# One decoder layer: work taken off VectorE, the way into the recurrence reordered, and a norm by ln and exp

## What is computed

```python
def rms_norm(x, gain):
    y = x * lax.rsqrt(jnp.mean(x * x, axis=-1, keepdims=True) + EPS)
    return y * gain
...
def step(S, inp):                       # one chunk of the recurrence, 8 heads
    qc, kc, vc, lc = inp
    b = jnp.cumsum(lc, axis=2)
    o = jnp.einsum('bhtd,bhde->bhte', qc * jnp.exp(b), S)
    ...
    o = o + jnp.einsum('bhts,bhse->bhte', a, vc)
    S = jnp.exp(b_last)[..., None] * S + jnp.einsum('bhsd,bhse->bhde', kc * jnp.exp(b_last[:, :, None] - b), vc)
...
def mixer_out(o_att, o_hg, og, attn_gain, hg_gain, w_out, dtype):
    a = rms_norm(o_att.reshape(B, T, ATT_WIDTH), attn_gain)
    h = rms_norm(o_hg, hg_gain).reshape(B, T, HG_WIDTH) * jax.nn.silu(og)
    return jnp.concatenate([a, h], axis=-1) @ w_out
```

## Time and profile before

| | |
|---|---|
| median of 3 runs | 2861.77 us (2860.55 to 2863.96) |
| time of the profiled execution | 2865.61 us, span 2863.9 us |
| TensorE busy | 2788.0 us (97%) |
| VectorE busy | 1472.6 us (51%) |
| ScalarE busy | 1007.2 us (35%) |
| GpSimd busy | 89.5 us (3%) |
| granted TensorE clock, mean | 0.988 |

### The profile page before, as it was taken

How to read it: one execution, slowest core, us unless ns; L and a number is a source line. 1 busy time by engine, 2 the same in 40 slices (tenths; PEclk the granted TensorE clock), 3 DMA queues, 4 the chain that set the end, 5 groups by cost and what they waited for, 6 DMA issues and landing times.

```text
span 2863.9 us, 50898 instructions
## 1 busy us (share of the span) xinstructions
PE 2788.0 (97%) x20916; PEld 2672.8 (93%) x20916; DVE 1472.6 (51%) x1854; ACT 1007.2 (35%) x1150; POOL 89.5 (3%) x161
## 2 busy tenths in 40 slices
PE   7999999999999999999999998999999999999999
PEld 5779999999999999998887787799999999999999
DVE  3434444434444444456666678875444434444433
ACT  3434333222233233333332344444333223222222
POOL 1110000000000010100000000020000000000000
PEclk9999999999999999999999998999999999999999
DMA  6365555455555454643336643445554456555454
GB/s 225 89 202 147 149 146 169 132 150 167 152 152 148 127 163 147 221 142 108 116 112 207 213 157 127 152 139 173 156 146 143 135 148 177 146 146 146 131 150 138
DMA packets 631369, 436.23 MB, mean 152 GB/s; under 512 B 14605, under 2 KB 615869, under 8 KB 623998
## 3 DMA queue, kind: packets, MB, share of 16 engines
q1 hardware_dynamic: 627746, 417.25, 48.2%
q0 software_dynamic: 2384, 14.11, 1.4%
q10 hardware_dynamic: 1100, 2.91, 0.3%
HBM read 421.16 MB, written 21.32 MB: 154 GB/s over the span
## 4 chain that ended last, share of the span: by engine, by line
PE 91%; DVE 5%; ACT 2%; issue 2%; DMA 0%; SPq 0%; POOLq 0%; POOL 0%; ACTq 0%; DVEq 0%
PE bank L409 65%; PE bank L763 12%; PE bank L1767 2%; PE bank L687 2%; PE bank L689 2%; PE bank L688 2%; ACT whi L742 1%; PE bank L1387 1%; DVE ors_h L2007 1%; DVE wlo L747 1%; PE bank L1175 1%; PE bank L1333 1%; ACT sc L1251 0%; PE bank L1176 0%; PE bank L1191 0%
## 5 line engine op out<-in xcount | busy, mean ns | idle before, releaser
L314 DVE TENSOR_TENSOR wlo<-wraw,whi 128x2048 fp32r<-128x2048 f32 (+1 forms) x305 | 612.7, 2009 | 508.9 <-ACT whi L310 486.0
L310 ACT ACTIVATE whi<-wraw 128x2048 fp32r<-128x2048 f32 (+1 forms) x305 | 513.3, 1683 | 679.2 <-PE bank L409 679.2
L409 PE MATMUL bank<-xl,whi 128*128 128x320 f32 x2816 | 441.8, 309 | 0.0
L409 PE MATMUL bank<-xh,whi 128*128 128x320 f32 x2816 | 441.8, 309 | 0.0
L409 PE MATMUL bank<-xh,wlo 128*128 128x320 f32 x2816 | 441.6, 309 | 0.0
L409 PEld LDWEIGHTS bank<-xl,whi 128*128 128x128 f32 x2816 | 420.2, 188 | 0.2
L409 PEld LDWEIGHTS bank<-xh,whi 128*128 128x128 f32 x2816 | 420.1, 188 | 0.1
L409 PEld LDWEIGHTS bank<-xh,wlo 128*128 128x128 f32 x2816 | 420.2, 188 | 0.0
L409 PE MATMUL bank<-hl,whi 128*128 128x320 f32 x1408 | 227.3, 309 | 0.0
L409 PE MATMUL bank<-hh,whi 128*128 128x320 f32 x1408 | 227.3, 309 | 0.0
L409 PE MATMUL bank<-hh,wlo 128*128 128x320 f32 x1408 | 227.3, 309 | 0.0
(11 more groups left out here) (329 smaller groups left out, 2653.5 us busy)
## 6 DMA issues: line engine op xcount, KB each, us to landing
wraw<-in_w_ffn_gate_up SPq DMA_DIRECT2D x176, 1024.0 KB, 5.5
wraw<-in_w_ffn_down SPq DMA_DIRECT2D x128, 704.0 KB, 4.5
wraw<-in_w_mix SPq DMA_DIRECT2D x52, 1024.0 KB, 4.8
...
```

The costliest lines, as they stand in the source:

```text
L310: act.activation(whi[:, a % 2, 0:size], wraw[:, a % RAW, 0:size], ACT.Copy).then_inc(s["hi_ready"], 1)
L314: dve.tensor_tensor(wlo[:, a % 2, 0:size], wraw[:, a % RAW, 0:size], whi[:, a % 2, 0:size].bitcast(F32), ALU.subtract).then_inc(s["lo_read ...
L409: mm = pe.matmul(b, w[:, a % 2, c], x[:, kk, :], start=first, stop=end)
```

## The change

What it does, in the order of the program:

- `values`: the four blocks of 32 output rows become two of 64, so each sequence has 52 matmuls in place of 104.
- The squares of the attention tiles are taken in two parts: the first 312 tokens as soon as the sequence before the last has its output, the last 8 for all tiles in one instruction at the end. There are eight buffers `osq` now. The reciprocal root is `Ln` and `Exp` with scale -0.5, both on ScalarE.
- `PRELUDE`: six runs of output tiles 0 and 1 stand ahead of the first beat; for these two tiles the lo weights come before the lo features. `RUNS` holds the other 42. VectorE makes xl before `dve_decayed(0)`, ScalarE makes xh before `act_decays(0)`.
- A chunk's output is copied by ScalarE (`act_results`), its state faded by GpSimd (`pool_state`); a head's output is copied by ScalarE (`act_head_copy`), its state faded and its gate applied by GpSimd (`pool_head`, `pool_head_gate`).
- Each head's norm is `Ln` and `Exp` on ScalarE, with no reciprocal on VectorE.

The diff, without its context lines and 8 spaces of indent:

```diff
@@ before, line 223
-osq = at("osq", 70.125, [P, 2, T])
+osq = at("osq", 56.125, [P, 8, T])
@@ before, line 1096
-RUNS = [(1, 1), (1, 2)] * 4 + [(1, 2), (0, 1)] + [(1, 1)] * 8 + [(0, 4), (0, 4)]
-FIRST_RUN = [sum(sum(r) for r in RUNS[:b]) for b in range(BEATS + 1)]
-OUT_AT = {b: -(-FIRST_RUN[b] // 3) for b in range(BEATS) if -(-FIRST_RUN[b] // 3) * 3 < FIRST_RUN[b + 1]}
+PRELUDE = [(0, 0), (0, 2), (1, 0), (1, 2), (0, 1), (1, 1)]
+RUNS = [(1, 1)] * 4 + [(1, 1), (1, 2)] * 2 + [(1, 1), (0, 0)] + [(1, 1)] * 8 + [(0, 3), (0, 3)]
+FIRST_RUN = [len(PRELUDE) + sum(sum(r) for r in RUNS[:b]) for b in range(BEATS + 1)]
+OUT_AT = {b: [i for i in range(2, KT) if FIRST_RUN[b] <= 3 * i < FIRST_RUN[b + 1]] for b in range(BEATS)}
+OUT_AT[0] = [1] + OUT_AT[0]
@@ before, line 1129
-        if b in OUT_AT and OUT_AT[b] + 5 < N_OUT:
-            i = OUT_AT[b]
-            if i == 0:
-                out_load(sp, 4)
+        if b == 0:
+            for i in (4, 5):
+                out_load(sp, i)
+        for i in OUT_AT.get(b, ()):
@@ before, line 1383
-                for r0 in range(0, P, 32):
-                    r, d0, q0 = slice(r0, r0 + 32), g2 * P + r0, 64 * g2 + 32 * (r0 // 64)
-                    lhs = s_v[:, kt, d0:d0 + 32] if kt < 12 else vnb[:, d0:d0 + 32]
+                for par in range(2):
+                    r, d0, q0 = slice(64 * par, 64 * par + 64), g2 * P + 64 * par, 64 * g2 + 32 * par
+                    lhs = s_v[:, kt, d0:d0 + 64] if kt < 12 else vnb[:, d0:d0 + 64]
@@ before, line 1701
+T_LAST = T - TS
+
@@ before, line 1702
+    act.wait_ge(s["s_o"], 4 * NB - 3)
@@ before, line 1704
-        if x >= 2:
-            act.wait_ge(s["o_ss"], x - 1)
-        act.activation(osq[:, x % 2, :], mixed(x), ACT.Square).then_inc(s["o_sq"], 1)
-    act.wait_ge(s["o_ss"], 8)
-    act.activation(ort[:, :], bank[7][:, 0:T], ACT.Sqrt, scale=1.0 / 1024, bias=eps_c[:, 0:1]
+        act.activation(osq[:, x, 0:T_LAST], mixed(x)[:, 0:T_LAST], ACT.Square).then_inc(s["o_sq"], 1)
+    act.wait_ge(s["s_o"], 4 * NB + 1)
+    act.activation(osq[:, :, T_LAST:T], q2[:, :, :, T_LAST:T].rearrange("p a h t -> p (a h) t"), ACT.Square
+                   ).then_inc(s["o_sq"], 1)
+    act.wait_ge(s["o_ss"], 9)
+    act.activation(ort[:, :], bank[7][:, 0:T], ACT.Ln, scale=1.0 / 1024, bias=eps_c[:, 0:1]
@@ before, line 1709
+    act.wait_ge(s["o_rt"], 1)
+    act.activation(ors[:, :], ort[:, :], ACT.Exp, scale=-0.5).then_inc(s["o_rs"], 1)
@@ before, line 1714
-        pe.matmul(bank[7][:, 0:T], ones[:, :], osq[:, x % 2, :], start=x == 0, stop=x == 7
+        pe.matmul(bank[7][:, 0:T_LAST], ones[:, :], osq[:, x, 0:T_LAST], start=x == 0, stop=x == 7
@@ before, line 1715
+    pe.wait_ge(s["o_sq"], 9)
+    for x in range(8):
+        mm = pe.matmul(bank[7][:, T_LAST:T], ones[:, :], osq[:, x, T_LAST:T], start=x == 0, stop=x == 7)
+    mm.then_inc(s["o_ss"], 1)
@@ before, line 1718
-    dve.wait_ge(s["o_rt"], 1)
-    dve.reciprocal(ors[:, :], ort[:, :]).then_inc(s["o_rs"], 1)
@@ before, line 1755
+    last = 1 if i < 2 else 2
@@ before, line 1768
-                       stop=run == 2 and k == 7)
-    if run == 2:
+                       stop=run == last and k == 7)
+    if run == last:
@@ before, line 1776
+def pe_prelude(pe):
+    for i, run in PRELUDE:
+        pe_out_run(pe, i, run)
+
@@ before, line 1903
+def act_results(act, c):
+    act.wait_ge(s["h_op"], c + 1)
+    act.activation(proj[:, T_HI:T_HI + HG, chunk(c)], bank[5][:, :].rearrange("p (h t) -> p h t", h=HG), ACT.Copy
+                   ).then_inc(s["h_o"], 1)
+
+def pool_state(pool, c):
+    pool.wait_ge(s["h_op"], c + 1)
+    pool.wait_ge(s["h_ebc"], c + 1)
+    pool.wait_ge(s["h_st"], c)
+    if c == 1:
+        pool.wait_ge(s["seg_set"], 4)
+    else:
+        pool.wait_ge(s["h_faded"], c - 1)
+    pool.tensor_tensor(st[:, :, :], st[:, :, :], ebc[:, c, :].unsqueeze(2).to_broadcast([P, HG, P]), ALU.mult
+                       ).then_inc(s["h_faded"], 1)
+
@@ before, line 1906
-    dve.wait_ge(s["h_op"], c + 1)
-    dve.tensor_copy(proj[:, T_HI:T_HI + HG, chunk(c)], bank[5][:, :].rearrange("p (h t) -> p h t", h=HG)
-                    ).then_inc(s["h_o"], 1)
@@ before, line 1910
-        dve.wait_ge(s["h_ebc"], c + 1)
-        link(dve.tensor_tensor(st[:, :, :], st[:, :, :], ebc[:, c, :].unsqueeze(2).to_broadcast([P, HG, P]),
-                               ALU.mult))
+        dve.wait_ge(s["h_faded"], c)
@@ before, line 1931
-            pe.wait_ge(s["h_zero"], 1)
+            pe.wait_ge(s["seg_set"], 4)
@@ before, line 1963
-    if h == 0:
-        dve.wait_ge(s["h_ebc"], NC + 1)
-    wait_state(dve, h)
-    dve.wait_ge(s["h_so"], h + 1)
-    dve.tensor_copy(proj[:, T_HI + h, TP:T], head_bank(h)).then_inc(s["h_oe"], 1)
-    link(dve.tensor_tensor(slot[:, :, :], slot[:, :, :], ebl[:, h, :].unsqueeze(2).to_broadcast([P, NB, P]), ALU.mult))
+    dve.wait_ge(s["h_faded"], NC - 1 + h + 1)
@@ before, line 1974
+def pool_head(pool, h):
+    slot = s0[h % SLOTS]
+    if h == 0:
+        pool.wait_ge(s["h_ebc"], NC + 1)
+    wait_state(pool, h)
+    pool.wait_ge(s["h_so"], h + 1)
+    pool.wait_ge(s["h_faded"], NC - 1 + h)
+    if h >= 3:
+        pool.wait_ge(s["o_ap"], 8 + h - 2)
+    pool.tensor_tensor(slot[:, :, :], slot[:, :, :], ebl[:, h, :].unsqueeze(2).to_broadcast([P, NB, P]), ALU.mult
+                       ).then_inc(s["h_faded"], 1)
+
+def pool_head_gate(pool, h):
+    if h == 0:
+        pool.wait_ge(s["h_sg"], 3)
+    pool.wait_ge(s["o_rs"], 1 + h + 1)
+    pool.wait_ge(s["h_faded"], NC - 1 + min(h + 3, HG))
+    if h:
+        pool.wait_ge(s["o_ap"], 8 + h)
+    o = mixed(8 + h)
+    pool.tensor_tensor(o, o, proj[:, T_HG + h, :], ALU.mult).then_inc(s["o_ap"], 1)
+
+def act_head_copy(act, h):
+    act.wait_ge(s["h_so"], h + 1)
+    act.activation(proj[:, T_HI + h, TP:T], head_bank(h), ACT.Copy).then_inc(s["h_oe"], 1)
+
@@ before, line 1989
-        act.wait_ge(s["o_ss"], 8 + h - 1)
+        act.wait_ge(s["o_ss"], 9 + h - 1)
@@ before, line 1993
-    pe.wait_ge(s["o_sq"], 8 + h + 1)
+    pe.wait_ge(s["o_sq"], 9 + h + 1)
@@ before, line 1995
-        pe.wait_ge(s["o_rt"], 1 + h - 1)
+        pe.wait_ge(s["o_rt"], 1 + 2 * (h - 2) + 1)
@@ before, line 1999
-    act.wait_ge(s["o_ss"], 8 + h + 1)
+    act.wait_ge(s["o_ss"], 9 + h + 1)
@@ before, line 2002
-    act.activation(ort_h[:, h % 2, :], bank[3 + h % 2][:, 0:T], ACT.Sqrt, scale=1.0 / P, bias=eps_c[:, 0:1]
+    act.activation(ort_h[:, h % 2, :], bank[3 + h % 2][:, 0:T], ACT.Ln, scale=1.0 / P, bias=eps_c[:, 0:1]
@@ before, line 2003
+    act.wait_ge(s["o_rt"], 1 + 2 * h + 1)
+    act.activation(ors_h[:, h % 2, :], ort_h[:, h % 2, :], ACT.Exp, scale=-0.5).then_inc(s["o_rt"], 1)
@@ before, line 2006
-    dve.wait_ge(s["o_rt"], 1 + h + 1)
-    dve.reciprocal(ors_h[:, h % 2, :], ort_h[:, h % 2, :]).then_inc(s["o_rs"], 1)
-    dve.wait_ge(s["o_rs"], 1 + h + 1)
+    dve.wait_ge(s["o_rt"], 1 + 2 * h + 2)
@@ before, line 2010
-    link(dve.scalar_tensor_tensor(out=o, in0=o, scalar=gain_hg[:, h:h + 1], in1=ors_h[:, h % 2, :],
-                                  op0=ALU.mult, op1=ALU.mult))
-    dve.tensor_tensor(o, o, proj[:, T_HG + h, :], ALU.mult).then_inc(s["o_ap"], 1)
+    dve.scalar_tensor_tensor(out=o, in0=o, scalar=gain_hg[:, h:h + 1], in1=ors_h[:, h % 2, :],
+                             op0=ALU.mult, op1=ALU.mult).then_inc(s["o_rs"], 1)
@@ before, line 2021
+    pe_prelude(pe)
@@ before, line 2049
-    act.wait_ge(s["s_o"], 4 * NB + 1)
@@ before, line 2050
+    act_out(act, 1)
+    for x in range(8):
+        act_mixed_hi(act, x)
@@ before, line 2054
-    for x in range(8):
-        act_mixed_hi(act, x)
@@ before, line 2057
-        if b in OUT_AT:
-            act_out(act, OUT_AT[b] + 1)
+        for i in OUT_AT.get(b, ()):
+            act_out(act, i + 1)
@@ before, line 2065
+                act_results(act, b // 2)
@@ before, line 2067
-                act.activation(flat(proj[:, T_HG:T_HG + HG, :]), flat(proj[:, T_HG:T_HG + HG, :]), ACT.Silu)
+                act.activation(flat(proj[:, T_HG:T_HG + HG, :]), flat(proj[:, T_HG:T_HG + HG, :]), ACT.Silu
+                               ).then_inc(s["h_sg"], 1)
@@ before, line 2072
+            act_head_copy(act, b - 11)
@@ before, line 2099
-    dve_decayed(dve, link, 0)
+    dve_out(dve, 1)
@@ before, line 2101
+    dve_decayed(dve, link, 0)
@@ before, line 2108
-        if b in OUT_AT:
-            i = OUT_AT[b]
-            if i:
-                dve_out_evict(dve, i - 1)
+        for i in OUT_AT.get(b, ()):
+            dve_out_evict(dve, i - 1)
@@ before, line 2140
-    pool.memset(vt[64:P, 2, :], 0.0).then_inc(s["h_zero"], 1)
+    pool.memset(vt[64:P, 2, :], 0.0).then_inc(s["seg_set"], 1)
+    for c in range(1, NC):
+        pool_state(pool, c)
+    for b in range(HG + 2):
+        if b < HG:
+            pool_head(pool, b)
+        if b >= 2:
+            pool_head_gate(pool, b - 2)
```

## The result

The changed kernel is faster, by less than forecast: 2849.63 us (2844.69 to 2850.29, 5 runs) for 2863.96 us of the kernel before, ratio 0.9937 with a 95% interval of 0.9925 to 0.9950. By the ratio that is 18 us less, between 14 and 21.5; the two medians lie 14.3 us apart. Measured again later beside other runs of the kernel before, the ratio was 0.9933 (0.9919 to 0.9946). The forecast was 36 us less, 2826 us; the measured median lies 0.6 us outside its range. The profiled execution took 2844.69 us, its span is 2843.0.

The account below looks back on a forecast made before the run. TensorE, busy for 97% of the span, was taken as the bound. Terms 2 to 4 gave -16.9 us, with term 5 -16.3, with term 1 -36: 2861.8 - 36 = 2826 us, range 2811 to 2849.

Parts of the forecast that it names:

- Term 1: Sequences' values in blocks of 64 rows: all 19.9 us of instruction stalls won, wider blocks costing 0.
- Terms 2 to 4: Passage, recurrence and heads together: 142.3 us for 159.2, 16.9 us less.
- Passage: Last values to the recurrence: 19 us, before 15.8 with none of the six output runs done.
- Recurrence: Stretch of 74.8 us before: 62.3 us, including 4 for hand-overs and 2 for half clock.
- Heads: Stretch of 68.6 us before: 61 us, with ScalarE late next at 6.85 us in a middle beat.
- Term 5: FFN2's first root needs a table load again: between 0 and 1.3 us, taken as 0.6.
- The values win nothing: Rival: stalls stay at other block edges or 64 columns cost more; 2846 us; 12%.
- GpSimd's lock: Rival: GpSimd and VectorE work follows each other in heads and recurrence, 12 us back, 2838 us; 15%.
- Table loads cost twice: Rival: a pause of 1.28 us behind each of 16 loads, 20.5 us back, 2846 us; 4%.
- Slower: Rival: heads' chain and lock; slower from a GpSimd fading of 5.8 us, 2875 us at 7; 5%.

Follow-up runs that it names:

- e4: Changed kernel with the 52 value matmuls reordered, all 13 key tiles of one 64-row block and then of the other: 2868.38 us, ratio 1.0012 to the kernel before.
- e6: Changed kernel with VectorE's eviction of output tile 0 moved ahead of chunk 1's decays: 2845.10 us, ratio 0.9935 to the kernel before.
- e7: Changed kernel with the fading of the states (three chunks, eight heads) back on VectorE, gates still on GpSimd: 2852.30 us, ratio 0.9963 to the kernel before.

## Why the prediction was wrong

**Term 1: the stalls right, the price wrong.** The stalls were what the records said, and all of them went. The step that failed is "The bounds for eight sequences are thus -9 and +12 us; I take 0". Measured: (3.16 - 1.89) x 8 = +10.2 us, close to the bound from the row of L1810 in the earlier trace rows. That row had the same 64 columns of weights and was the only one shown with them; it should have been taken. The argument "half the records take half the time" leaves out that a record's price hangs on what stands beside it (e4). With +10 the forecast would have been 2836. The rule of the Trainium skill (Runtime: NRT & Kernel Launch, Instruction fetch mechanics) that fetching is hidden is against these traces: with 32 rows the waits without a releaser are 14.7 and 16.3 us, always near multiples of 256 records apart.

**Terms 2 to 4: the sum 142.3 us, measured 149.4** (21.4, 64.5 and 63.6), and 0.8 us more in the second half, which began at the half clock. With the 10 us of term 1 these 8 make up the distance between 36 and the 19.4 us of the two traces. The mechanisms were right and the sizes small, each by 2 to 3 us. The median missed the forecast by 24 us. The stages account for 17 of them; 2 more are that the kernel before measured 2863.96 us here for 2861.77, and the rest is within the spread of single executions (2844.69 to 2850.29).
- *Passage, 21.4 for 19.* The prediction's own terms add up to 19.3 (9.7 + 3.7 + 5 x 1.175). The first output run came 10.8 us behind the values for 9.7: the sums took 6.1 us for 5.3, and `ohi` of 1.04 us stands ahead of the first `xh`. The rest is the half clock after TensorE's wait of 3.80 us: 10.6 us from the first output run to the scores for 9.6 (3.7 and 5 x 1.175).
- *Recurrence, 64.5 for 62.3.* 4 us for hand-overs and 2 for the clock were guesses. One hand-over made nearly all of it, the eviction (e6), which the prediction doesn't name anywhere among VectorE's instructions. Without it the stretch is 58.4 us, near the 56.4 of TensorE's own work. That all idle time and half clock of the kernel before would go was taken without asking what caused them; the cause of most of it, the wait for `kst`, was one that the change does remove.
- *Heads, 63.6 for 61.* ScalarE as the bound and its beat of 6.85 us are right (6.73, as between `vm` at 1816.37 and 1823.09), the loads of 1.28 with no pause too. It was busy for 56.0 us where 54.4 were counted, and idle for 7.6 where its ends were taken as 4 and 2.3. TensorE waited 2.41 us for `vm`, 2.9 for the additions and 4.0 for the last `xh`.
- *Term 5* was taken as 0.6 and is 0: FFN2 lasts 933.1 us in both.

**The rivals.** *The values win nothing*: no, but the row that it rested on held. *GpSimd's lock*: a fading took 1.90 us in seven of eleven cases and 2.2 to 2.95 in the others, not 2.8 or 3.6 each time. The two engines do hold each other up; VectorE's `olo` and GpSimd's fading, in the recurrence:

```profile
1780.61 2.48 DVE L1754 TENSOR_TENSOR olo<-oraw,ohi 128x1024 fp32r<-128x1024 f32 x1
```

```profile
1780.11 1.90 POOL L1932 TENSOR_TENSOR st<-st,ebc 128x1024 f32<-128x1024 f32 x1 [12.81 <-PE bank L1829]
```

The fading began first and kept its 1.90 us; the `olo`, 1.22 us elsewhere, takes 2.48 and ends 1.08 behind it. In the heads an `olo` began 0.03 us ahead of a fading, took 1.23, and the fading took 2.95. It doesn't decide: with the fading on VectorE (e7) recurrence and heads are 3 us longer. *Table loads cost twice*: no pause in any row, the activation begins 0.02 us behind the load and the load 0.02 us behind the activation ahead of it; the drain of 1380 ns that the Trainium skill (ScalarE: Activation LUTs, What ACT_TABLE_LOAD costs) gives doesn't show here. Two loads per head stand in the rows, so its section Table sets, by which ln and exp need one, doesn't hold for this program. *Slower*: the fading would have had to last 5.8 us; the longest took 2.95.
